# Scaling a unit's first weight tile on ScalarE instead of GpSimd, behind the next unit's exponentials

## The reference

```python
# differential attention: two softmaxes, the second subtracted
p = softmax(s, axis=-1)                  # s: (b, h, c=2, q, k)
w = p[:, :, 0] - lam * p[:, :, 1]
out = einsum('bhqk,bkhe->bqhe', w, v)
# bidirectional mLSTM: a forward and a backward scan, added
s = einsum('bhtd,bhsd->bhts', q, k) * exp(dmat - m_t[..., None])
h = num / maximum(abs(den), exp(-m_t))[..., None]
yx = yx_f + flip(yx_b)
```

## Time and profile before

| | |
|---|---|
| median of 3 runs | 3029.94 us (3028.42 to 3035.05) |
| the profiled execution | 3029.98 us, of which the span is 3028.2 us |
| TensorE busy | 2893.2 us, 96% |
| VectorE busy | 1945.6 us, 64% |
| ScalarE busy | 1152.7 us, 38% |
| GpSimd busy | 338.4 us, 11% |
| mean granted clock of TensorE | 0.975 |
| L1298 on GpSimd | 32 instructions, 39.8 us, from 514.1 to 716.3 us |

### The profile page before, as it was taken

How to read it: one execution, slowest core, us unless ns; L and a number is a source line. 1 busy time by engine, 2 the same in 40 slices (tenths; PEclk the granted TensorE clock), 3 DMA queues, 4 the chain that set the end, 5 groups by cost and what they waited for, 6 DMA issues and landing times.

```text
span 3028.2 us, 39339 instructions
## 1 busy us (share of the span) xinstructions
PE 2893.2 (96%) x15776; PEld 2404.1 (79%) x15776; DVE 1945.6 (64%) x3261; ACT 1152.7 (38%) x1901; POOL 338.4 (11%) x396
## 2 busy tenths in 40 slices
PE   7999999988999999999999999999989999998998
PEld 6888897545888888888887889976778888876898
DVE  7788855645687856878554765544466775457554
ACT  4222234443422224222254655434362223535552
POOL 0000010321100001000011120200130001200201
PEclk8999999978999999999999999999999999999999
DMA  6666522101455634556331245421134442343353
GB/s 237 221 217 230 182 87 83 42 28 42 147 201 196 214 104 172 199 199 212 108 123 64 77 146 183 158 77 39 59 112 167 168 152 91 94 100 86 132 187 107
DMA packets 126005, 412.28 MB, mean 136 GB/s; under 512 B 25296, under 2 KB 27472, under 8 KB 125312
## 3 DMA queue, kind: packets, MB, share of 16 engines
q1 hardware_dynamic: 110272, 353.14, 34.7%
q0 software_dynamic: 15552, 56.63, 5.3%
HBM read 408.67 MB, written 1.05 MB: 135 GB/s over the span
## 4 chain that ended last, share of the span: by engine, by line
PE 83%; DVE 6%; ACT 6%; POOL 2%; issue 2%; DMA 1%; SPq 0%; POOLq 0%; ACTq 0%; DVEq 0%
PE bank L2327 25%; PE bank L2329 25%; PE bank L2328 25%; PE bank L2571 2%; POOL sb_temp L1274 1%; ACT sb_split_high L1397 1%; DVE sb_split_low L1807 1%; DVE sb_h_low L1894 1%; DMA sb_na_raw<-na_rpb 1%; DVE sb_temp L1888 1%; PE bank L2719 1%; PE bank L2532 1%; ACT sb_x_res L1475 1%; ACT sb_temp L1458 0%; PE bank L2654 0%
## 5 line engine op out<-in xcount | busy, mean ns | idle before, releaser
L2327 PE MATMUL bank<-sb_h_high,sb_split_high 128*128 128x256 f32 (+1 forms) x3040 | 1048.8, 345 | 40.7 <-DVE sb_h_low L1902 17.9
L2328 PE MATMUL bank<-sb_h_low,sb_split_high 128*128 128x256 f32 (+1 forms) x3040 | 1028.8, 338 | 0.0
L2329 PE MATMUL bank<-sb_h_high,sb_split_low 128*128 128x256 f32 (+1 forms) x3040 | 1028.6, 338 | 0.0
L1807 DVE TENSOR_TENSOR sb_split_low<-sb_raw,sb_split_high 128x1024 fp32r<-128x1024 f32 x515 | 635.9, 1242 | 230.2 <-ACT sb_split_high L1397 227.3
L2327 PEld LDWEIGHTS bank<-sb_h_high,sb_split_high 128*128 128x128 f32 x3040 | 580.2, 191 | 131.2 <-DVE sb_h_low L1902 23.0
L1397 ACT ACTIVATE sb_split_high<-sb_raw 128x1024 fp32r<-128x1024 f32 x515 | 537.3, 1051 | 336.9 <-DMA sb_raw<-weights 336.9
L2328 PEld LDWEIGHTS bank<-sb_h_low,sb_split_high 128*128 128x128 f32 x3040 | 580.9, 191 | 64.1 <-issue 0.5
L2329 PEld LDWEIGHTS bank<-sb_h_high,sb_split_low 128*128 128x128 f32 x3040 | 580.3, 191 | 64.8
L1821 DVE CUSTOM_DVE_ANT_0 sb_temp<-sb_ada_ffn,sb_cond_ffn 128x1024 bf16<-128x1024 f32 x396 | 466.0, 1220 | 18.2 <-DMA sb_ada_ffn<-ada 9.8
L1951 DVE SCALAR_TENSOR_TENSOR sb_x_res<-bank,sb_gates,sb_x_res 128x256 f32<-128x256 f32 x320 | 145.1, 479 | 234.4 <-PE bank L2329 233.9
L2327 PE MATMUL bank<-sb_hidden_high_ffn,sb_split_high 128*128 128x512 f32 (+1 forms) x830 | 279.7, 337 | 0.0
(11 more groups left out here) (272 smaller groups left out, 3069.0 us busy)
## 6 DMA issues: line engine op xcount, KB each, us to landing
sb_raw<-weights SPq DMA_DIRECT2D x515, 512.0 KB, 3.3
sb_ada_ffn<-ada SPq DMA_DIRECT2D x114, 512.0 KB, 4.4
sb_ada_ffn<-ada POOLq DMA_DIRECT2D x90, 512.0 KB, 3.7
sb_ada_mlp<-ada POOLq DMA_DIRECT2D x18, 512.0 KB, 3.5
sb_ada_mlp<-ada SPq DMA_DIRECT2D x18, 512.0 KB, 4.2
sb_cond_ffn<-cond SPq DMA_DIRECT2D x3, 1024.0 KB, 5.3
sb_na_raw<-na_rpb SPq DMA_DIRECT2D x32, 96.0 KB, 6.0
sb_x_res<-tokens SPq DMA_DIRECT2D x4, 512.0 KB, 8.2
```

The lines of the kernel that those rows point to most:

```text
L1807: do.tensor_tensor(m.low[i][:, :], m.raw[i][:, :], m.high[i][:, :].bitcast(F32), ALU.subtract).then_inc(*dve.mark("split_low", s))
L2327: do.matmul(out, ah, bh, start=start and j == 0, stop=False)
L2328: do.matmul(out, ah, bl, start=False, stop=False)
L2329: last = do.matmul(out, al, bh, start=False, stop=stop and j == len(terms) - 1)
```

## The change

GpSimd's `first_scaled` and the two steps that call it go. ScalarE gets a `first_scaled` that does the same multiplication as an Identity activation with the column as its scale. It is a step of its own, `("first", kind, u)`, which `apart` puts behind the weights or scores of the turn in which unit u is normalised: in turn i, ScalarE takes the exponentials of unit i and then scales the first tile of unit i-1. Nothing else moves in the list.

```diff
-def apart(units, name):
+def apart(units, kind, name):
     for turn in units:
-        yield [s for s in turn if s[0] != name], [s for s in turn if s[0] == name]
+        yield [s for s in turn if s[0] != name], [s for s in turn if s[0] == name] + [
+            ("first", kind, s[1]) for s in turn if s[0] == f"{kind}_normalise"]
...
-    def first_scaled(kind, u, coef):
-        pair, n = m.temp[2 * (u % 3)], n_keys(u % TT)
-        do.tensor_scalar(pair[:, 0:n], pair[:, 0:n], coef, None, ALU.mult).then_inc(*pool.mark("first_scaled", (kind, u)))
-
-    def da_normalise(u):
-        pool.wait_ge("exped", ("da", u, 1))
-        pool.wait_ge("recip", ("da", u))
-        first_scaled("da", u, m.cols[u % 6][:, 4:5])
-
-    def ml_normalise(u):
-        pool.wait_ge("recip", ("ml", u))
-        first_scaled("ml", u, m.cols[u % 6][:, 6:7])
...
+    def first_scaled(kind, u):
+
+        first, n = m.temp[2 * (u % 3)], n_keys(u % TT)
+        act.wait_ge("recip", (kind, u))
+        do.activation(first[:, 0:n], first[:, 0:n], identity, scale=m.cols[u % 6][:, 4:5] if kind == "da" else m.cols[u % 6][:, 6:7]).then_inc(
+            *act.mark("first_scaled", (kind, u)))
```

More of the change, by code:

```diff
@@ L663, in even_steps @@
     more = lambda u: ((("weigh", "ml", u // TT),) if u % TT == TT - 1 else ())
-    units = list(apart(turns(4 * TT, ("ml_weights", "ml_normalise", "ml_combine", "ml_turn"), more), "ml_weights"))
+    units = list(apart(turns(4 * TT, ("ml_weights", "ml_normalise", "ml_combine", "ml_turn"), more), "ml", "ml_weights"))
     extra = [[] for _ in units]
@@ L676, in even_steps @@
     more = lambda u: ((("weigh", "da", u // TT), ("add_squares", "da", u // TT), ("sum_squares", "da", u // TT)) if u % TT == TT - 1 else ())
-    units = list(apart(turns(4 * TT, ("da_scores", "da_normalise", "da_combine", "da_turn"), more), "da_scores"))
+    units = list(apart(turns(4 * TT, ("da_scores", "da_normalise", "da_combine", "da_turn"), more), "da", "da_scores"))
     extra = [[] for _ in units]
@@ L1335, in pool_program @@
     work = {"ada": ada, "square": square, "add_mean": add_mean, "centre": centre,
-            "rope": rope, "da_normalise": da_normalise, "ml_normalise": ml_normalise, "even_norm": even_norm,
+            "rope": rope, "even_norm": even_norm,
             "gla_decay3": gla_decay3, "gla_factors": gla_factors, "plain": plain}
@@ L1741, in na_turn @@
         pair_turn("na", u, u // 2, 2 + u % 2, TT, NA_WT)
-    work = {"split": split, "split_high": split_high, "cond_silu": cond_silu, "cond_col": cond_col, "square": square, "first_square": first_square, "centre": centre, "small_square": small_square, "mean": mean,
+    work = {"first": first_scaled, "split": split, "split_high": split_high, "cond_silu": cond_silu, "cond_col": cond_col, "square": square, "first_square": first_square, "centre": centre, "small_square": small_square, "mean": mean,
             "scaled": scaled, "plain": plain, "plain_put": plain_put, "layer_norm": layer_norm, "silu": silu, "relu": relu,
```

## The result

| | before | after |
|---|---|---|
| median, 13 runs each | 3028.83 us (3025.51 to 3035.05) | 3039.15 us (3036.19 to 3041.42) |
| ratio | | 1.0030 [1.0022, 1.0038] |
| the profiled execution | 3029.98 us | 3039.84 us, of which the span is 3038.0 us |
| mean granted clock | 0.975 | 0.973 |

The changed kernel is 0.3% slower, by 10.3 us between the medians. The forecast of 3041.4 us is 2.2 us above the measured median.

What follows compares the result with a forecast made beforehand. TensorE, busy 96% of the span, was taken as the bound, with exposed units set by VectorE, ScalarE and TensorE. Queue terms of 10.7 us plus 0.8 of clock, 11.5 on 3029.98, gave 3041.4 us; range 3031 to 3050.

Steps and rivals of the forecast that it cites:

- Prices: ScalarE's scaling was taken at 0.70 us for 512 columns and 0.50 us for 256.
- Units 4 and 8: First loop: the bank copy that TensorE waits for comes later, +1.3 us in each of the two units.
- End of the first loop: Units 12 to 16: slips accumulate to 4.5 us, the shorter last scaling returns 0.9, so TensorE's turn is 3.6 us later.
- Second loop, units 3 to 6: Scalings and combinations delay exponentials and reciprocal; the even_norm product and TensorE's weighing at 661.46 come 2.5 us late.
- Units 7 to 10: Second loop: the late reciprocal delays TensorE, and unit 8 adds 0.4 and no more: 1.7 us.
- The full 1.27 us: Second loop: the reciprocal at 672.05 and TensorE at 673.12 get the whole delay of a late normalisation, 1.27 us.
- unit 8 added 0.9: Second loop: GpSimd's product, no longer behind the scaling, regains 1.0 us, so this unit was to add only 0.4 us.
- The last unit: End of the second loop: it adds 0.3 us.
- The clock: Both loops: longer TensorE waits bring slow stretches; half a stretch, 0.8 us, was taken, with bounds 0 and 7 us.
- The rival in which each region gets one of its own: Each of four regions brings its own low-clock stretch, 7 us instead of 0.8: 3048 us, chance 0.15.
- The swallowed slip: VectorE's idle time in tail and second loop absorbs the delay, leaving units 4 and 8, 2.6 us: 3032.6 us, chance 0.17.
- The late GpSimd: Combinations come no later in exposed units, so the waits for GpSimd go, 7 us gained: 3023 us, chance 0.08.

Runs made afterwards that it cites:

- the held GpSimd: Kernel before, with GpSimd's scaling placed later in its queue and waiting for the next unit's second exponential: 3059.28 us, ratio 1.0093, loops +29.6 us.
- the one with idle activations: Kernel before, GpSimd still scaling, plus 32 Identity activations on ScalarE at the change's place that nobody waits for: 3028.94 us, loops +0.6 us.

## Why the prediction was right

The mechanism is shown from four sides. The same instructions ahead of the exponentials cost nothing (-0.1 us); the same load on ScalarE without the wait costs 0.6 (both medians lie at or under that of the kernel before); GpSimd with the wait is slow too (+29.6, though its step also moved in GpSimd's queue), so it is not ScalarE; and with the normalisation taken out from behind the wait, the two kernels are equal (+6.2 both, medians 3033.95 and 3034.12 us). From the first unit to the last turn of the first loop the changed kernel is 6.8 us later and from there to the end of the second 3.9, where I had 6 and 4 to 5.

*Prices.* I took 0.70 and 0.50 us for ScalarE's scaling; the rows show 0.715 and 0.500. By the Trainium skill, ScalarE: Activation LUTs, section What ACT_TABLE_LOAD costs, an ACTIVATE with one pointer operand takes 280 ns plus 0.833 ns a column, 707 and 493 ns here; the trace agrees.

*Units 4 and 8*, 1.3 us each. TensorE's waits were to be 1.6 and 3.1 us and are 1.65 and 3.11. Unit 4 cost 1.2. Unit 8 cost 1.6, the 1.3 of the queue and about 0.35 of low clock behind the longer wait.

*End of the first loop*, 3.6 us, measured 4.0. The replay through the queues holds step by step: counted from unit 8, the scores at 599.66 come 2.0 us late, the combination of 601.25 3.4, that of 605.24 4.9 and the last turn 4.0, where I had 2.2, 3.6, 4.5 and 3.6. The part that I had not put there is the clock. The weighing of the third head took 3.94 us for 2.75, 1.2 us more, and the last exponentials stand in ScalarE's queue behind the copy of it (L1589):

```profile
609.78 0.73 DVE L2096 TENSOR_TENSOR sb_temp<-bank,sb_ml_masks 128x256 f32<-128x256 f32 x2
...
610.37 0.60 ACT L1589 ACTIVATE sb_even_big<-bank 128x512 f32<-128x512 f32 x1 [2.56 <-PE bank L2566]
```

The first of the two masks (0.40 us) is done at 610.18, the exponential starts at 610.86. So at most 0.7 of the 1.2 us reached the path; the rest lay beside VectorE's slip. The two windows over that weighing:

```profile
600.70:603.80 3.10, 3.10 (x12) 1.75 (x12) 2.60 (x11) 1.78 (x6) 0.67 (x2) 1.00 0.00 0
```

```profile
606.30:610.40 4.10, 4.10 (x11) 1.99 (x10) 2.73 (x10) 1.54 (x6) 0.00 (x0) 0.70 0.00 0
```

Before, the granted clock is 1.00 (2.4 GHz throughout); after, 0.70, a mixture of the two levels, behind a wait of 2.96 us for L2106 at 604.62 where it had been 2.54.

*Second loop, units 3 to 6*, 2.5 us, measured 2.2. *Units 7 to 10*, 1.7 us, measured 1.0, which is 2.2 in the queues less 1.16 that the clock gave back in the weighing. The full 1.27 us at TensorE's row product is there (its wait behind L2129 at 682.40 grew from 2.93 to 4.21 us), and unit 8 added 0.9 where I had 0.4:

```profile
670.63 4.33 PE L2566 MATMUL bank<-sb_even_big 128*128 128x512 f32 x8 [2.88 <-DVE sb_even_big L2129]
...
682.40 2.07 PE L2601 MATMUL bank<-sb_even_big,sb_const 8*128 8x512 f32 x2 [4.21 <-DVE sb_even_big L2129]
...
682.50 1.26 POOL L1303 TENSOR_TENSOR sb_even_big<-sb_even_big 128x512 f32<-128x512 f32 x1 [10.51 <-DVE sb_even_big L2129]
...
685.66 0.76 DVE L2066 TENSOR_REDUCE sb_cols<-bank 128x1 f32<-128x256 f32 x2 [0.45 <-PE bank L2500]
```

The weighing took 5.49 us in the earlier trace rows, all of it at 0.50, and now runs at a mean of 0.65. Unit 8 is a term that I had too small: GpSimd's product does win the 0.9 us, since it follows L2129 at once (682.50), but the next maxima (L2066) then wait 0.45 us for TensorE's scores, which stand behind the late row product. Less than half of what was regained got through. *The last unit*, 0.3 us, measured 0.65.

*The clock*, 0.8 us in all, was not there: about +0.7 and +0.35 in the first loop and -1.16 in the second, so -0.1 net. Unit 4, where I had expected a low stretch, has none. The queues alone cost 11.0 us for the 10.7 that I had summed; that the clock's losses and its gain cancel was luck. I had called the prediction wrong if the second loop's stretch at low clock were shorter; it is not: over 50 us (645 to 695 before, 651.7 to 701.7 after) the mean granted clock is 0.66 in both, and only the weighing's place in it moved. The rival in which each region gets one of its own (3048 us) fell. The swallowed slip (3032.6 us) fell too: the tail and the second loop pay 7.9 us. The late GpSimd (3023 us) fell because the combinations come later, not sooner; and with no scaling at all the median wins 4.5 us and the one trace 0.8, not 7.

Open remain the 4.5 us in the median of the kernel without scaling, of which its one trace shows 0.8, and how the +29.6 us of the held GpSimd divide.

## What to carry to other kernels

An instruction moved to an idle engine costs by where it stands in that engine's queue and by what is queued behind whoever waits for it. Ask of each consumer what it used to overlap with: here the combination had run for free beside an exponential, and a producer placed behind that exponential took the cover away, for 0.66 us of VectorE plus 0.6 of ScalarE in every exposed unit. The same producer one place earlier cost nothing in sum.

## What the runs showed of the hardware

The weighing of a head, 4 matmuls that a row counts as x8, took 2.75 us at a granted clock of 1.00, 3.94 at 0.70, 4.44 at 0.62, 4.93 at 0.55 and 5.49 at 0.50. The 3.94 and the 4.93 us are the same head behind the same instructions in the same order, in the changed kernel and in the one changed in the first loop only. So a small saving or loss upstream can be amplified or undone by up to 2 us at each such place, which is as much as the whole effect of the smaller edits here.

Two executions of kernels with the same work can differ by 3.4 us in one part that no edit touched: over 1620 to 1660 us the granted clock was 0.83 in the kernel before and 0.91 in the one with idle activations, in these rows.

```profile
1620.00:1660.00 40.00, 32.48 (x157) 26.23 (x156) 13.88 (x25) 16.81 (x29) 1.91 (x3) 0.83 0.19 66
```

```profile
1620.00:1660.00 40.00, 32.48 (x181) 27.03 (x180) 17.05 (x31) 16.82 (x29) 2.56 (x4) 0.91 0.18 66
```
